# Paged decode attention: the four key blocks of a group on four sets of 32 array columns

## The chip, the cores and the metric

The program runs on one core of one Trainium2 chip. The metric is device time in microseconds for the whole program, the median of the runs; smaller is better. TensorE, VectorE, ScalarE and GpSimd are called PE, DVE, ACT and POOL as in the profile. A matmul holds one operand in the array (the weights, up to 128 columns of them) and streams the other through it; PEld is the loading of the weights.

## What is computed

The program is one inference step of a small decoder: a DeltaNet layer, a latent-attention layer, and an expert layer behind each. The change is in one part of the attention layer, the decode: eight requests, each with one new token, attend over 4096 cached keys that lie in pages. In the reference's terms, for one request (the key's normalising factor `kscale` and the token's own key are folded in by the kernel):

```python
PAST_LEN = 4096; MLA_HEADS = 8; KV_LORA = 256; ROPE_DIM = 64
cache_latent  # pages of (PAGE_SIZE, 256) latents
cache_krope   # pages of (PAGE_SIZE, 64) rotated keys
cache_kscale  # pages of (PAGE_SIZE, 8) per-row per-head factors
# per head h, with the query taken into latent space:
# score[t, h] = (qlat[h] . latent[t] + qrope[h] . krope[t]) * kscale[t, h] * SOFTMAX_SCALE
# p = softmax over the 4096 past tokens and the token itself
# o[h] = sum_t p[t, h] * latent[t]          (256 values, later times w_uv)
```

All of it is float32.

## The kernel before

Everything that matters here is in `mla_dec`. A request's cache is gathered by three indirect DMAs of POOL (line 1651): `c` (the latents, 128 partitions x 32 blocks x 256), `kr` (32 blocks x 64) and `ks`. There are two buffers of each (index `a`), so a gather fills the buffer of the request after the next. The 32 blocks of 128 keys are worked through in eight groups of four (`BQ = 4`, `NG = 8`).

PE's program is written out by hand in `turn` and `step`. Step g of a request does, in this order:

- `flips`: ten 128x128 transposes that turn the latents (lines 1720, 1721) and the rotated keys (line 1725) of group g. ACT and DVE copy the results from PSUM to `cT` and `rT` (lines 1682, 1683, 1903).
- `scores` for group g-1: the weights are the queries, 8 columns wide (`ql`, `qr`), and the streamed operand is `cT` or `rT`. Line 1731 streams all four blocks at once, 512 columns, twice (two halves of the latent); line 1733 streams 256 columns twice. The scores land in `pL` as 8 partitions x 512. DVE copies them to `lines` (line 1851).
- `back` for group g-2: four small transposes (line 1739) bring `lines` into `pS`, keys on partitions.

The softmax of the request before is spread over the steps of this one: `largest`, `over_all`, `lowered`, `summed` and `divided` on DVE, `maximum` and `spread_maximum` on PE, `soften` on ACT. Behind step 4 comes `values` (line 1774): 32 matmuls, the weights `S` 8 columns wide, each streaming 256 columns of `c`, all summed into the same 8 partitions of `pO`. ACT copies them to `vs` (line 1676) in step 6, and `sums` turns them behind step 7 (lines 1779, 1781).

Two waits tie this to the gathers. POOL may refill `c` only when `values` has read it, and PE may start a request only when its latents have landed:

```python
                        apart(pool, at("pv", i - 1, a + 1))
                        gather(a, latents)
...
                    if g == 0:
                        after(pe, (s[f"lc{a}"], i * 16 + 16), (s[f"lr{a}"], i * 16 + 16))
```

The first of these lines stands behind the `kr` and `ks` gathers in POOL's loop. `values` of request r runs in step 4 of request r+1, and it is request r+2 that needs the buffer.

Of the kernel before, what the change touches and what calls it, by code (L numbers as in the profile page):

```python
# [23 lines left out]
ALU = mybir.AluOpType  # L24
ACT = mybir.ActivationFunctionType
AX = mybir.AxisListType
F32 = mybir.dt.float32
U32 = mybir.dt.uint32
ds = bass.ds

P = 128
# [6 lines left out]
H = 8  # L38
# [4 lines left out]
QL, KL, RD = 512, 256, 64  # L43
# [4 lines left out]
PER = PAST // P  # L48
# [9 lines left out]
C_ID, C_ONE, C_UP, C_STRICT, C_NEG, C_LEVEL = 0, 1, 2, 3, 4, 5  # L58
# [149 lines left out]
def part(tile, n, width):  # L208

    dims = " ".join("abcd"[:len(tile.shape) - 1])  # L210
    flat = tile[:].rearrange(f"p {dims} -> p ({dims})") if len(tile.shape) > 2 else tile
    return flat[:, ds(n * width, width)]
# [1360 lines left out]
def mla_dec(core, q, ckvT, krTs, ksc, wuv, os):  # L1573
# [6 lines left out]
    nc = core.nc  # L1580
    N = NS * H
    BQ = 4
    NG = PER // BQ
    T0 = SEQ
    TURNS = NS // 2
    with Marks(core, "pag", inp=96, step=15, turned=1, lat_made=1, self_made=1,
               idx=2, lc0=16, lc1=16, lr0=16, lr1=16, lk0=16, lk1=16,
               flip=2 * NG, half0=2 * NG, half1=2 * NG, keyr=2 * NG, dotted=2 * NG, lined=2 * NG, staged=4, scored=2, soft0=10, soft1=10, maxed=2, spread=2, exped=4,
               pv=2, v_out=2, v_turned=2, o=6, final=1) as s, ExitStack() as ctx:
# [6 lines left out]
        c = [core.sbuf(ctx, "c", [P, PER, KL]) for _ in range(2)]  # L1596
# [3 lines left out]

        qr2 = core.sbuf(ctx, "qr2", [P, NS + 1, 2, H])
        qlat = core.sbuf(ctx, "qlat", [P, 2, NS + 1, H])
        ql = [core.sbuf(ctx, "ql", [P, 2, H]) for _ in range(2)]
        qr = [core.sbuf(ctx, "qr", [P, 2, H]) for _ in range(2)]
        lines = [core.sbuf(ctx, "lines", [H, BQ, P]) for _ in range(2)]
        prod = core.sbuf(ctx, "prod", [P, 3, NS, H])
        spread = core.sbuf(ctx, "spread", [NS, NS, H])
        sself = core.sbuf(ctx, "sself", [P, N])
        krep = core.sbuf(ctx, "krep", [P, N])
        cT = [core.sbuf(ctx, "cT", [P, 2, BQ, P]) for _ in range(2)]  # L1610
        rT = [core.sbuf(ctx, "rT", [P, BQ // 2, P]) for _ in range(2)]
        S = [core.sbuf(ctx, "S", [P, PER, H]) for _ in range(2)]
        m = [core.sbuf(ctx, "m", [P, 6, H]) for _ in range(2)]
        mx = [core.sbuf(ctx, "mx", [H, 1 + H]) for _ in range(2)]
        vs = core.sbuf(ctx, "vs", [H, KL])
        olat = core.sbuf(ctx, "olat", [P, 2, NS, H])
        b0 = [core.psum(ctx, "b0", [P, BQ, P]) for _ in range(2)]
        b1 = [core.psum(ctx, "b1", [P, BQ, P]) for _ in range(2)]
        b2 = core.psum(ctx, "b2", [P, BQ // 2, P])
        pS = core.psum(ctx, "pS", [P, PER, H])  # L1620
        pL = core.psum(ctx, "pL", [P, BQ, P])
        pMO = core.psum(ctx, "pMO", [P, P + 4 * H + KL])
        pM, pO = pMO[:, 0:P + 4 * H], pMO[:, P + 4 * H:]
        M_SPREAD, M_SUM, M_VALUE = (slice(P + k * H, P + (k + w) * H) for k, w in ((0, 1), (1, 1), (2, 2)))

        def flat(tile):
            return tile[:, :, :].rearrange("p a b -> p (a b)")
# [10 lines left out]
        with nc.Block() as block:  # L1638
# [9 lines left out]
            def _(pool):  # L1648
# [9 lines left out]
                with pool.Fori(1, TURNS) as i:  # L1658
                    for a in range(2):
                        apart(pool, at("idx", i, a + 1), at("flip", i - 1, NG * (a + 1)))  # L1660
                        gather(a, keys)
# [5 lines left out]
            @block.scalar  # L1667
            def _(act):
                def soften(i, a):
                    after(act, at(f"soft{a}", i, 7))  # L1670
                    act.activation(S[a][:, :, :], S[a][:, :, :], ACT.Exp).then_inc(s["exped"], 1)
                    act.activation(m[a][:, 3, :], m[a][:, 2, :], ACT.Exp).then_inc(s["exped"], 1)  # L1672

                def value_out(i, a):
                    after(act, at("pv", i, a + 1), at("v_turned", i, a))
                    act.activation(vs[:, :], pO[:H, :], ACT.Copy).then_inc(s["v_out"], 1)

                def turn(i, first):
                    for a in range(2):
                        for g in range(NG):  # L1680
                            after(act, at("flip", i, NG * a + g + 1))
                            act.activation(cT[g % 2][:, 0, :, :], b0[g % 2][:, :, :], ACT.Copy).then_inc(s["half0"], 1)  # L1682
                            act.activation(rT[g % 2][:, :, :], b2[:, :, :], ACT.Copy).then_inc(s["keyr"], 1)
                            if a or not first:
                                if g == 3:
                                    soften(*before(i, a))
                                if g == 6:
                                    value_out(*before(i, a))

                turns(act, turn)  # L1690
                soften(TURNS - 1, 1)
                value_out(TURNS - 1, 1)

            @block.tensor
            def _(pe):
# [4 lines left out]
                for h in range(H):  # L1700
                    pe.transpose(pS[:, h, :], q[:NS, NT, h, QK - P:QK], eye)
                    last = pe.transpose(pS[:RD, H + h, :], q[:NS, NT, h, HD:QK], eye)
                last.then_inc(s["turned"], 1)
                pe.wait_ge(s["step"], 8)
                for h in range(H):
                    for e in range(2):
                        last = pe.matmul(pO[:, e * N + NS * h:e * N + NS * h + NS], wukT[:, h, P * e:P * e + P], qnT[:, h, :], start=True, stop=True)
                last.then_inc(s["lat_made"], 1)
                pe.wait_ge(s["step"], 14)
                own = pS[:, 0:NS, :].rearrange("p b h -> p (b h)")  # L1710
                pe.matmul(own, core.ones, prod[:, 0, :, :].rearrange("p b h -> p (b h)"), start=True, stop=False)
                pe.matmul(own, core.ones, prod[:, 1, :, :].rearrange("p b h -> p (b h)"), start=False, stop=False)
                pe.matmul(own, core.ones[:RD, :], prod[:RD, 2, :, :].rearrange("p b h -> p (b h)"), start=False, stop=True)
                pe.matmul(pM[:, 0:N], core.ones[:NS, :], spread[:, :, :].rearrange("p b h -> p (b h)"), start=True, stop=True).then_inc(s["self_made"], 1)
                pe.wait_ge(s["step"], 16)

                def flips(i, a, g):

# [3 lines left out]
                    if g or a or not isinstance(i, int):  # L1722
                        after(pe, at("keyr", i, NG * a + g))
                    for j in range(BQ // 2):
# [3 lines left out]
                def scores(a, g):  # L1728

                    for e in range(2):  # L1730
                        pe.matmul(pL[:H, :, :].rearrange("p j c -> p (j c)"), ql[a][:, e, :], cT[g % 2][:, e, :, :].rearrange("p j c -> p (j c)"), start=e == 0, stop=False)  # L1731
                    for e in range(2):
                        last = pe.matmul(pL[:H, e:BQ:2, :], qr[a][:, e, :], rT[g % 2][:, :, :], start=False, stop=e == 1)  # L1733
                    last.then_inc(s["dotted"], 1)

                def back(g):

                    for j in range(BQ):
                        last = pe.transpose(pS[:, BQ * g + j, :], lines[g % 2][:, j, :], core.const[:H, C_ID, 0:H])
                    return last  # L1740

                def step(i, a, g, first):

# [27 lines left out]
                def values(i, a):  # L1771
                    after(pe, at("exped", i, 2 * a + 2), at("v_out", i, a))
                    for j in range(PER):
                        last = pe.matmul(pO[:H, :], S[a][:, j, :], c[a][:, j, :], start=j == 0, stop=j == PER - 1)  # L1774
                    last.then_inc(s["pv"], 1)

                def sums(i, a):
                    after(pe, at(f"soft{a}", i, 8), at("v_out", i, a + 1))
                    pe.matmul(pM[:, M_SUM], core.ones, m[a][:, 4, :], start=True, stop=True)
                    for e in range(2):  # L1780
                        last = pe.transpose(pM[:, P + (2 + e) * H:P + (3 + e) * H], vs[:, P * e:P * e + P], core.const[:H, C_ID, 0:H])
                    last.then_inc(s["v_turned"], 1)

                def turn(i, first):
# [15 lines left out]
                for h in range(H):  # L1800
                    for e in range(2):
                        last = pe.matmul(pO[:, NS * h:NS * h + NS], wuv[:, e, HD * h:HD * h + HD], olat[:, e, :, h], start=e == 0, stop=e == 1)
# [3 lines left out]
            def _(dve):  # L1806
                done = [0]

                def then(ins):
                    ins.then_inc(s["step"], 1)  # L1810
                    done[0] += 1
                    dve.wait_ge(s["step"], done[0])
# [5 lines left out]
                then(dve.memset(qr2[:, :, :, :], 0.0))  # L1818
                then(dve.memset(qlat[:, :, :, :], 0.0))
                then(dve.memset(ptf[:, :], 0.0))  # L1820
                dve.wait_ge(s["inp"], 96)
                then(dve.tensor_copy(ptf[:, 0:NS], ptab[:, :]))

# [18 lines left out]

                def stage(v, a):

                    dve.tensor_copy(ql[a][:, :, :], qlat[:, :, ds(v, 1), :].rearrange("p e o h -> p e (o h)")).then_inc(s["staged"], 1)
                    dve.tensor_copy(flat(qr[a]), part(qr2, v, 2 * H)).then_inc(s["staged"], 1)

                def line(i, n):

                    after(dve, at("dotted", i, n))  # L1850
                    dve.tensor_copy(lines[(n - 1) % 2][:, :, :], pL[:H, :, :]).then_inc(s["lined"], 1)  # L1851

                def soft(a, ins):
                    ins.then_inc(s[f"soft{a}"], 1)
# [242 lines left out]
```

## Time and profile before

| what | value |
|---|---|
| median of 3 runs | 4729.99 us (4720.45 to 4735.25) |
| span of the profiled execution | 4702.6 us |
| what lies around the span (median less span) | 27.4 us |
| decode attention in the trace | about 2650 to 3088 us |
| its loop over steps | 2676.5 to 3087.4 us |
| PE busy, whole span | 81% |

The profile gives the span from the first to the last instruction; its execution has no other time of its own, so the metric stands 27.4 us above the span by the median. The share of PE is an average over stages with different limits; the decode attention is one of them, and the rows further down are all from it but the first.

### The profile page before, as it was taken

The numbers are of one execution on the slowest core, as the hardware profiler recorded it, in microseconds if no ns is written. First come the engines' busy times: TensorE is split into PE (matmuls) and PEld (weight loads), VectorE is DVE, ScalarE is ACT, GpSimd is POOL, SyncE is SP. The second block draws the span as 40 slices with busy tenths as digits, with TensorE's granted clock in tenths as the row PEclk, the third lists the DMA queues.
The fourth block names the chain that finished last, engine by engine and source line by source line (L and its number), as shares of the span: only waits on it lengthen the run. The fifth ranks groups of instructions, "written<-read, shape, count | busy, mean of one in ns | idle before, by whom it ended". The sixth has DMA issues, their size and how long they took to land. (4 is left out here: it accounts for less than half of the span.)

```text
span 4702.6 us, 43808 instructions
## 1 busy us (share of the span) xinstructions
PE 3830.8 (81%) x12357; PEld 1998.9 (43%) x12357; DVE 2699.2 (57%) x6392; ACT 951.4 (20%) x2394; POOL 1397.7 (30%) x1188
## 2 busy tenths in 40 slices
PE   7977888788788778787787799987887887877877
PEld 6866674433333333333244544434333333333332
DVE  2423452777777777777334332216777777777773
ACT  2212331121221222212113211102222122121220
POOL 0002340344434444444100000003444444444442
PEclk9987888899989999999799899998999999998988
DMA  2221001899999999999510222217999999999996
GB/s 88 74 57 31 3 1 41 330 392 371 399 371 378 395 381 373 395 376 391 210 52 1 101 102 92 81 40 310 383 371 392 377 371 391 368 379 382 373 387 258
DMA packets 200755, 1207.37 MB, mean 257 GB/s; under 512 B 28936, under 2 KB 48656, under 8 KB 65056
## 3 DMA queue, kind: packets, MB, share of 16 engines
q0 software_dynamic: 152448, 1133.58, 60.3%
q1 hardware_dynamic: 48160, 72.24, 4.6%
q8 instruction: 42, 0.69, 0.1%
q14 instruction: 105, 0.86, 0.0%
HBM read 1197.88 MB, written 7.86 MB: 256 GB/s over the span
## 5 line engine op out<-in xcount | busy, mean ns | idle before, releaser
L1172 PE MATMUL po<-ring,diag 128*128 128x512 f32 x4096 | 2031.2, 650 | 572.8 <-ACT diag L1037 572.4
L994 POOL DMA_INDIRECT ring<-in_uv,idx x1024 | 1226.8, 1198 | 1960.5 <-PE po L1172 1451.0
L1083 DVE SCALAR_TENSOR_TENSOR ring<-ring,xn 128x1024 f32<-128x1024 f32 x1024 | 1224.6, 1224 | 512.4 <-DMA ring<-in_uv,idx 472.4
L1172 PEld LDWEIGHTS po<-ring,diag 128*128 128x128 f32 x4096 | 819.4, 207 | 1612.5 <-issue 953.4
L1032 ACT ACTIVATE hg<-hs 128x4 f32<-128x4 f32 x256 | 52.6, 206 | 1979.6 <-DVE ring L1083 1979.6
L1037 ACT ACTIVATE diag<-gated,hg 128x128 f32<-128x128 f32 x1024 | 327.2, 390 | 15.6 <-ACT hg L1032 8.9
L1132 PE MATMUL pq<-xnT,w 128*128 128x512 f32 (+1 forms) x512 | 260.5, 594 | 1.5 <-ACT q L1012 1.5
L269 PE MATMUL acc<-xnT,w 128*128 128x260 f32 x1024 | 227.9, 385 | 5.1 <-ACT inp L305 4.2
L269 PEld LDWEIGHTS acc<-xnT,w 128*128 128x128 f32 x1024 | 194.8, 191 | 37.7 <-ACT inp L305 6.6
L1059 DVE TENSOR_TENSOR gated<-const,gate 128x2048 f32<-128x2048 f32 x64 | 146.8, 2293 | 2.2
L1133 PEld LDWEIGHTS pqs<-xnT,w 128*128 128x128 f32 x512 | 97.4, 190 | 115.9 <-issue 107.5
L499 POOL TENSOR_TENSOR gU<-const,cols 128x512 f32<-128x512 f32 x8 | 8.4, 1044 | 445.0 <-POOLq L130 418.4
L1903 DVE COPY cT<-b 128x512 f32<-128x512 f32 x64 | 44.3, 692 | 142.7 <-PE b L1725 142.7
L1132 PEld LDWEIGHTS pq<-xnT,w 128*128 128x128 f32 x512 | 90.8, 191 | 82.5 <-issue 82.5
L1731 PE MATMUL pL<-cT,ql 128*8 128x512 f32 x256 | 121.6, 598 | 0.0
L1851 DVE COPY lines<-pL 8x512 f32<-8x512 f32 x64 | 43.5, 679 | 127.7 <-PE pL L1733 127.7
L1774 PE MATMUL pMO<-c,S 128*8 128x256 f32 x512 | 113.5, 383 | 1.3 <-ACT m L1672 1.3
L882 DVE MAX8 sv<-pS 128x8 f32<-128x128 f32 x128 | 31.6, 289 | 136.2 <-issue 88.7
L1483 POOL COPY knh<-kn 128x512 f32 x8 | 4.9, 612 | 334.7 <-SPq L1476 243.6
L1682 ACT ACTIVATE cT<-b 128x512 f32<-128x512 f32 x64 | 38.1, 595 | 322.2 <-PE b L1725 322.2
L1016 ACT ACT_TABLE_LOAD x64 | 82.1, 1283 | 94.5 <-DVE tab L908 92.0
L1075 DVE TENSOR_TENSOR x<-po,x 128x1024 f32<-128x1024 f32 x64 | 78.1, 1221 | 17.5 <-PE po L1172 17.5
(436 smaller groups left out, 4200.4 us busy)
## 6 DMA issues: line engine op xcount, KB each, us to landing
w<-in_w_gdn SPq DMA_DIRECT2D x32, 512.0 KB, 3.5
w<-in_w_peer SPq DMA_DIRECT2D x32, 512.0 KB, 7.8
ring<-in_uv,idx POOLq DMA_INDIRECT x1024, 8.8
S<-in_state_ssm SPq DMA_DIRECT2D x16, 256.0 KB, 3.1
out_ssm_s<-S SPq DMA_DIRECT2D x16, 256.0 KB, 3.2
w<-in_w_gdn_out SPq DMA_DIRECT2D x2, 2048.0 KB, 13.4
w<-in_w_mla_out SPq DMA_DIRECT2D x2, 2048.0 KB, 12.9
wq<-in_w_uq SPq DMA_DIRECT2D x1, 3072.0 KB, 15.5
```

The source lines that it names most:

```text
L269: last = pe.matmul(acc[c % 2][:, r, :], w[:, c, k, :], xnT[:, k, PART * r:PART * r + PART], start=k == 0, stop=k == KD - 1)
L994: pool.indirect_dma_start(out=ring[:, c % RING, :], out_offset=None, in_=uv, in_offset=bass.IndirectOffsetOnAxis(ap=idx[t % 2][:, c:c + 1] ...
L1016: act.activation(k.e[:, :], k.tv[:, :], ACT.Exp, bias=k.low[:, 0:1], accum_out=k.z[:, 0:1]).then_inc(s["exped"], 1)
L1037: act.activation(diag[:, c % RING, :], gated[a][:, c, :], ACT.Copy, scale=hg[a][:, c:c + 1]).then_inc(s["diag"], 1)
L1059: dve.tensor_tensor(gated[b][:, :, :], core.const[:, C_ID:C_ID + 1, :].to_broadcast([P, TOPK, P]), gate[:, :].rearrange("p (c o) -> p c o" ...
L1075: dve.tensor_tensor(core.x[:, t, :], po[t % 2][:, :], core.x[:, t, :], ALU.add).then_inc(s["added"], 1)
L1083: dve.scalar_tensor_tensor(ring[:, c % RING, 0:D], ring[:, c % RING, 0:D], 1.0, xn[:, t, :], ALU.mult, ALU.mult, accum_out=hs[a][:, c:c + ...
L1132: pe.matmul(pq[:, start:], w[:, p, j, :], xnT[:, j, start:SEQ], start=j == 0, stop=j == KD - 1)
L1133: last = pe.matmul(pqs[:, :], w[:, p, j, :], xnT[:, j, SEQ:ROWS], start=j == 0, stop=j == KD - 1)
L1172: last = pe.matmul(po[a][:, HALF * e:HALF * e + HALF], diag[:, c % RING, :], ring[:, c % RING, D + HALF * e:D + HALF * e + HALF], start=c ...
L1731: pe.matmul(pL[:H, :, :].rearrange("p j c -> p (j c)"), ql[a][:, e, :], cT[g % 2][:, e, :, :].rearrange("p j c -> p (j c)"), start=e == 0, ...
L1774: last = pe.matmul(pO[:H, :], S[a][:, j, :], c[a][:, j, :], start=j == 0, stop=j == PER - 1)
```

## The change

`ql` and `qr` become 32 columns wide, with zeros behind the 8 queries. Each of the four blocks of a group gets its own matmul with 128 streamed columns, and its output goes to its own 32 partitions of `pL`, which takes its own 32 columns of the array. `pL` and `lines` are now 128 partitions x 128. The four transposes of `back` become one matmul, with the 128x128 `lines` as weights and 32 columns of the identity streamed. `values` adds blocks 0, 4, 8, ... into partitions 0 to 7, blocks 1, 5, ... into 32 to 39, and so on; `vs` has 128 partitions, and `sums` adds the four parts by a matmul with `pick`, a 0/1 matrix. A setup matmul gives all of `pO` a finite value.

```diff
-        ql = [core.sbuf(ctx, "ql", [P, 2, H]) for _ in range(2)]
-        qr = [core.sbuf(ctx, "qr", [P, 2, H]) for _ in range(2)]
-        lines = [core.sbuf(ctx, "lines", [H, BQ, P]) for _ in range(2)]
+        ql = [core.sbuf(ctx, "ql", [P, 2, COLS]) for _ in range(2)]
+        qr = [core.sbuf(ctx, "qr", [P, 2, COLS]) for _ in range(2)]
+        lines = [core.sbuf(ctx, "lines", [P, P]) for _ in range(2)]
+        pick = core.sbuf(ctx, "pick", [P, COLS])
...
-                    act.activation(vs[:, :], pO[:H, :], ACT.Copy).then_inc(s["v_out"], 1)
+                    act.activation(vs[:, :], pO[:, :], ACT.Copy).then_inc(s["v_out"], 1)
...
+                pe.matmul(pO[:, :], core.ident, core.const[:, C_ID:C_ID + 2, :].rearrange("p a c -> p (a c)"), start=True, stop=True)
...
                     for e in range(2):
-                        pe.matmul(pL[:H, :, :].rearrange("p j c -> p (j c)"), ql[a][:, e, :], cT[g % 2][:, e, :, :].rearrange("p j c -> p (j c)"), start=e == 0, stop=False)
-                    for e in range(2):
-                        last = pe.matmul(pL[:H, e:BQ:2, :], qr[a][:, e, :], rT[g % 2][:, :, :], start=False, stop=e == 1)
+                        for j in range(BQ):
+                            pe.matmul(pL[COLS * j:COLS * j + COLS, :], ql[a][:, e, :], cT[g % 2][:, e, j, :], start=e == 0, stop=False)
+                    for j in range(BQ):
+                        last = pe.matmul(pL[COLS * j:COLS * j + COLS, :], qr[a][:, j % 2, :], rT[g % 2][:, j // 2, :], start=False, stop=True)
...
-                    for j in range(BQ):
-                        last = pe.transpose(pS[:, BQ * g + j, :], lines[g % 2][:, j, :], core.const[:H, C_ID, 0:H])
-                    return last
+                    return pe.matmul(pS[:, BQ * g:BQ * g + BQ, :], lines[g % 2][:, :],
+                                     core.ident.rearrange("p (j c) -> p j c", c=COLS)[:, :, 0:H], start=True, stop=True)
...
                     for j in range(PER):
-                        last = pe.matmul(pO[:H, :], S[a][:, j, :], c[a][:, j, :], start=j == 0, stop=j == PER - 1)
+                        b = COLS * (j % BQ)
+                        last = pe.matmul(pO[b:b + H, :], S[a][:, j, :], c[a][:, j, :], start=j < BQ, stop=j >= PER - BQ)
...
                     for e in range(2):
-                        last = pe.transpose(pM[:, P + (2 + e) * H:P + (3 + e) * H], vs[:, P * e:P * e + P], core.const[:H, C_ID, 0:H])
+                        last = pe.matmul(pM[:, P + (2 + e) * H:P + (3 + e) * H], vs[:, P * e:P * e + P], pick[:, 0:H], start=True, stop=True)
...
+                for a in range(2):
+                    then(dve.memset(ql[a][:, :, :], 0.0))
+                    then(dve.memset(qr[a][:, :, :], 0.0))
+                then(dve.tensor_reduce(pick[:, :], core.ident.rearrange("p (j c) -> p c j", c=COLS), AX.X, ALU.add))
...
-                    dve.tensor_copy(lines[(n - 1) % 2][:, :, :], pL[:H, :, :]).then_inc(s["lined"], 1)
+                    dve.tensor_copy(lines[(n - 1) % 2][:, :], pL[:, :]).then_inc(s["lined"], 1)
```

On PE, at the end of a step 4, the order of before is this. A row gives the line, the output and the inputs, the output's shape, and how often it follows in a row; `pMO` holds `pO`.

```order
L1725 MATMUL b_313<-const,kr 128x128 x2
L1731 MATMUL pL<-cT,ql 8x512 x2
L1733 MATMUL pL<-rT,qr 8x2x128 x2
L1739 MATMUL pS<-const,lines 128x8 x4
L1774 MATMUL pMO<-c,S 8x256 x32
L1720 MATMUL b_310<-const,c 128x128
```

The same place of the changed program, where the line numbers have moved by three or four:

```order
L1728 MATMUL b_314<-const,kr 128x128 x2
L1735 MATMUL pL<-cT,ql 32x128 x8
L1737 MATMUL pL<-rT,qr 32x128 x4
L1742 MATMUL pS<-const,lines 128x32
L1778 MATMUL pMO<-c,S 8x256 x32
L1723 MATMUL b_311<-const,c 128x128
```

Nothing stands in another place than before: four score matmuls have become twelve shorter ones, four transposes one matmul, and the 32 of `values` are as many and as long as they were.

## Rows read from the trace of the kernel before

**Rows 1.** The page: span and busy time of the engines.

```profile
span 4702.6 us, 43808 instructions
PE 3830.8 (81%) x12357; PEld 1998.9 (43%) x12357; DVE 2699.2 (57%) x6392; ACT 951.4 (20%) x2394; POOL 1397.7 (30%) x1188
```

**Rows 2.** Stage windows: window, us, busy time by engine, granted clock, DMA share, GB/s.

```profile
2880.00:2930.00 50.00, 49.19 (x250) 22.85 (x249) 14.59 (x32) 7.62 (x19) 2.82 (x3) 1.00 0.28 107
```

**Rows 3.** Groups by line from 2676 to 3090 us: busy, mean ns | idle before.

```profile
L1731 PE MATMUL pL<-cT,ql 128*8 128x512 f32 x256 | 121.6, 598 | 0.0
L1774 PE MATMUL pMO<-c,S 128*8 128x256 f32 x512 | 113.5, 383 | 1.3 <-ACT m L1672 1.3
L1733 PE MATMUL pL<-rT,qr 128*8 128x256 f32 x256 | 65.7, 379 | 0.0
L1739 PE MATMUL pS<-const,lines 8*128 8x8 f32 x256 | 26.3, 207 | 0.4 <-DVE lines L1851 0.4
```

**Rows 4.** Timeline of one step: start, us, engine, line, operation.

```profile
2861.86 0.33 PE L1720 MATMUL b<-const,c 128*128 128x128 f32 x1
2862.79 0.38 PE L1725 MATMUL b<-const,kr 128*128 128x128 f32 x2
2863.11 1.88 PE L1731 MATMUL pL<-cT,ql 128*8 128x512 f32 x4
2863.54 0.09 PEld L1731 LDWEIGHTS pL<-cT,ql 128*8 128x8 f32 x1 [0.34 <-issue]
2863.71 0.38 ACT L1683 ACTIVATE rT<-b 128x256 f32<-128x256 f32 x1
2864.83 1.03 PE L1733 MATMUL pL<-rT,qr 128*8 128x256 f32 x4
2865.78 0.41 PE L1739 MATMUL pS<-const,lines 8*128 8x8 f32 x4
2865.89 0.68 DVE L1851 COPY lines<-pL 8x512 f32<-8x512 f32 x1 [1.98 <-PE pL L1733]
2866.12 0.33 PE L1720 MATMUL b<-const,c 128*128 128x128 f32 x1
```

**Rows 5.** Timeline from values to the next request's first transpose.

```profile
2785.75 8.15 PE L1774 MATMUL pMO<-c,S 128*8 128x256 f32 x37
2793.83 0.33 PE L1720 MATMUL b<-const,c 128*128 128x128 f32 x1
...
2806.61 0.39 PE L1779 MATMUL pMO<-m,const 128*128 128x8 f32 x2
2806.93 0.29 PE L1781 MATMUL pMO<-const,vs 8*128 8x8 f32 x2
...
2807.79 0.33 PE L1720 MATMUL b<-const,c 128*128 128x128 f32 x1 [0.57 <-DMA c<-in_cache_latent,idx]
```

**Rows 6.** POOL's timeline: first and last of six latent gathers.

```profile
2745.10 0.94 POOL L1651 DMA_INDIRECT c<-in_cache_latent,idx  x1 [25.31 <-PE pMO L1774]
...
2993.56 0.94 POOL L1651 DMA_INDIRECT c<-in_cache_latent,idx  x1 [25.32 <-PE pMO L1774]
```

**Rows 7.** Waits, 2676 to 3090 us: total us, times, longest.

```profile
PE b L1720 <- DMA c<-in_cache_latent,idx: 5.2, 6, 1.1
```

**Rows 8.** Timeline and a window behind a clock drop.

```profile
3007.15 0.33 PE L1720 MATMUL b<-const,c 128*128 128x128 f32 x1 [1.05 <-DMA c<-in_cache_latent,idx]
3008.98 2.93 PE L1731 MATMUL pL<-cT,ql 128*8 128x512 f32 x4
...
3009.00:3011.00 2.00, 2.00 (x4) 0.35 (x4) 0.69 (x1) 0.87 (x2) 0.00 (x0) 0.50 0.00 0
```

**Rows 9.** Timeline: first step, and the last values.

```profile
2659.01 0.17 DVE L1822 CAST ptf<-ptab 128x8 f32<-128x8 int32 x1 [7.64 <-DMA wukT<-in_w_ukT]
2676.53 0.45 PE L1720 MATMUL b<-const,c 128*128 128x128 f32 x1 [3.44 <-DMA kr<-in_cache_krope,idx]
...
3065.35 15.67 PE L1774 MATMUL pMO<-c,S 128*8 128x256 f32 x64 [1.34 <-ACT m L1672]
```

More of the change, by code:

```diff
@@ L1582, in mla_dec @@
     BQ = 4
+    COLS = P // BQ
     NG = PER // BQ
@@ L1585, in mla_dec @@
     TURNS = NS // 2
-    with Marks(core, "pag", inp=96, step=15, turned=1, lat_made=1, self_made=1,
+    with Marks(core, "pag", inp=96, step=17, turned=1, lat_made=1, self_made=1,
                idx=2, lc0=16, lc1=16, lr0=16, lr1=16, lk0=16, lk1=16,
@@ L1614, in mla_dec @@
         mx = [core.sbuf(ctx, "mx", [H, 1 + H]) for _ in range(2)]
-        vs = core.sbuf(ctx, "vs", [H, KL])
+        vs = core.sbuf(ctx, "vs", [P, KL])
         olat = core.sbuf(ctx, "olat", [P, 2, NS, H])
@@ L1620, in mla_dec @@
         pS = core.psum(ctx, "pS", [P, PER, H])
-        pL = core.psum(ctx, "pL", [P, BQ, P])
+        pL = core.psum(ctx, "pL", [P, P])
         pMO = core.psum(ctx, "pMO", [P, P + 4 * H + KL])
@@ L1703, in _ @@
                 last.then_inc(s["turned"], 1)
-                pe.wait_ge(s["step"], 8)
+                pe.wait_ge(s["step"], 13)
                 for h in range(H):
@@ L1708, in _ @@
                 last.then_inc(s["lat_made"], 1)
-                pe.wait_ge(s["step"], 14)
+                pe.wait_ge(s["step"], 19)
                 own = pS[:, 0:NS, :].rearrange("p b h -> p (b h)")
@@ L1714, in _ @@
                 pe.matmul(pM[:, 0:N], core.ones[:NS, :], spread[:, :, :].rearrange("p b h -> p (b h)"), start=True, stop=True).then_inc(s["self_made"], 1)
-                pe.wait_ge(s["step"], 16)
+                pe.wait_ge(s["step"], 21)
+                pe.matmul(pO[:, :], core.ident, core.const[:, C_ID:C_ID + 2, :].rearrange("p a c -> p (a c)"), start=True, stop=True)
                 def flips(i, a, g):
@@ L1843, in stage @@
                 def stage(v, a):
-                    dve.tensor_copy(ql[a][:, :, :], qlat[:, :, ds(v, 1), :].rearrange("p e o h -> p e (o h)")).then_inc(s["staged"], 1)
-                    dve.tensor_copy(flat(qr[a]), part(qr2, v, 2 * H)).then_inc(s["staged"], 1)
+                    dve.tensor_copy(ql[a][:, :, 0:H], qlat[:, :, ds(v, 1), :].rearrange("p e o h -> p e (o h)")).then_inc(s["staged"], 1)
+                    dve.tensor_copy(qr[a][:, :, 0:H], qr2[:, ds(v, 1), :, :].rearrange("p o e h -> p (o e) h")).then_inc(s["staged"], 1)
                 def line(i, n):
                     after(dve, at("dotted", i, n))
-                    dve.tensor_copy(lines[(n - 1) % 2][:, :, :], pL[:H, :, :]).then_inc(s["lined"], 1)
+                    dve.tensor_copy(lines[(n - 1) % 2][:, :], pL[:, :]).then_inc(s["lined"], 1)
                 def soft(a, ins):
```

## Prediction

> **What bounds it now.** I read the page first: PE is busy for 81% of the span [rows 1]. That is an average, so I turned to the decode attention, the only place that the change touches. In its windows PE is busy for 49.2 of 50 us at full clock (1.00, which is 2.4 GHz), while DMA moves data for 28% of the time [rows 2]. The groups by line show on what: lines 1731, 1774 and 1733 keep PE for 301 of the 414 us that the view covers [rows 3]. All three have weights only 8 columns wide, so most of the array has nothing to do in them. Those are the matmuls that the change spreads over the array.
>
> A step of four blocks repeats every 4.26 us (2861.86 to 2866.12) [rows 4]. Its parts, from start to start: ten transposes 1.25, line 1731 1.72, line 1733 0.95, `back` 0.34. The reader is to see two more things there. Each float32 matmul leaves two records with a load each (256 records of line 1731 for 128 matmuls, two in each of 64 steps), and a record of 512 columns takes 1.72 / 4 = 0.43 us: so 0.107 us for each 128 columns. And between the last transpose (2862.79 plus one pitch of 0.11 is 2862.90) and the first score matmul (2863.11) lie 0.21 us where the pitch of a transpose is 0.11: 0.10 us is lost where the array changes from 128 columns to a narrow set. `values` is 64 records of 256 columns, with a pitch of (8.15 - 0.38) / 36 = 0.216 us, 13.8 us for one request [rows 3, 5].
>
> The second limit is right behind PE. `values` ends at about 2793.83 with the first transpose behind it, and only then may POOL issue the gather that refills those latents [rows 5]. PE does three more steps and `sums`, and then waits 0.57 us for it [rows 5]; over the six such places it waits 5.2 us in all, 0.87 each [rows 7]. The gather fits almost exactly into three steps of today's length. From `values` to the next request's start it takes 13.96 + 0.30 = 14.26 us on average, whatever PE does. Six requests have this wait; they come (2993.56 - 2745.10) / 5 = 49.7 us apart [rows 6].
>
> **The change part by part.** Scores: 12 matmuls of 128 columns, 24 records of 0.107 us. If nothing overlaps that is 2.57 us, as now. If the four column sets run fully at once, it is 0.64. No row of this trace shows two sets at work together, so these are the bounds, and a third value lies between. The two records of one matmul go to the same columns, one behind the other, and the second has to wait until the first has streamed. If matmuls start in program order, the next block's first record can only overlap this second one. Then each matmul costs one record: 12 + 1 records, 1.39 us. I take this middle value, since all records of the trace start in order. With the 0.10 us of the change of shape that is 1.49 in place of 2.67.
>
> The Trainium skill ("TensorE: Matmul & The Clock Gate", Part 3: Packing small matmuls) has a measured 2.38x for three column tiles, and says that matmuls start and end strictly in program order. By its rate, carried on to four tiles (an estimate: 2.57 / 3.2), the scores would take about 0.8 us; by its order rule with two records to a tile, the 1.39 above. No run here shows either yet.
>
> A floor of issue is possible too: four pairs of load and matmul take 0.41 us in line 1739 with 0.207 for one, a pitch of 0.068 us [rows 3, 4]. With 128-column loads that would make 24 pairs 1.63 us; loads of 32 columns should be shorter, so it bounds the middle value from above and takes most of the difference between it and the best case away.
>
> `back`: two records with a 128-column load. The nearest row is line 1779, two such records, 0.32 us to the next line [rows 5]. In place of 0.34, no change. A step is then 1.25 + 1.49 + 0.32 = 3.06 us: 1.20 less.
>
> `values`: 32 matmuls, one record each exposed, 33 x 0.216 = 7.1 us in place of 13.8, 6.7 less (bounds: 64 / 4 records, 3.5 us, and nothing). `sums` gets two more records of line 1779's kind, 0.3 us a request [rows 5].
>
> DVE's copy of the scores reads 128 columns instead of 512, so it falls from 0.68 us towards 0.3 [rows 4]; that is off the path. A shorter step must still cover the copies: ACT's end at 2863.71 + 0.38 = 2864.09, 1.2 us behind the last transpose's start, and the next step's transposes of the keys and its scores need them some 2.7 us behind it, still in time [rows 4]. The setup's five DVE instructions stand ahead of a wait of 7.64 us for a DMA, and the extra matmul on `pO` ahead of PE's 3.44 us for the first keys [rows 9]; uncovered they would cost some 2 us once.
>
> Now the gather. Three steps and `sums` are 3 x 3.06 + 0.9 = 10.1 us, but the gather needs 14.26: PE waits 4.2 us at each of six requests. The period becomes 14.26 + 5 x 3.06 + 7.1 + 0.5 (the softmax's small matmuls, what is left of 49.7 by the same sum now) = 37.2 us. An idle PE also loses its clock. Once after a wait of 1.05 us it fell to 0.50 (1.2 GHz): the transposes took 1.83 us (3007.15 to 3008.98) instead of 1.25, and line 1731 2.93 instead of 1.88, 1.6 us lost; the last `values`, behind several short waits, took 15.67, 1.9 more than 64 x 0.216 [rows 4, 8, 9]. I add 1.8 us to each period: 39.0, or 10.7 us less than 49.7.
>
> The sum: six periods 64; from the first transpose (2676.53) to the first gather 13 steps and one `values`, 13 x 1.20 + 6.7 = 22; behind the last period four steps' worth of scores and the last `values`, 4 x 1.20 + 6.7 = 12 [rows 6, 9]. Together 98 us, less 1 for `sums` and setup: 97. The span goes from 4702.6 to 4606; with the 27.4 us around it, 4633 against the median of 4730. If PE alone set the end it would be 64 x 1.20 + 8 x 6.7 = 130; the gathers and the clock keep 33 back.
>
> **The rivals.**
>
> Full overlap: the column sets take two records each without holding up the rest. Step 2.31 us, `values` 3.5; period 14.26 + 11.6 + 3.5 + 0.5 + 1.8 = 31.6, 18 less; 6 x 18 + 13 x 1.95 + 10.3 + 4 x 1.95 + 10.3 = 162, so 4568. For it: nothing in the trace forbids it. Against: the two records of a matmul, and the 0.068 us pitch of pairs.
>
> No overlap: float32 matmuls run one after another wherever they land. Columns streamed are as many as now (512 x 2 + 256 x 2 a step; 256 x 32 in `values`), so the time stays: 4730, within 5 us. The step-by-step widths agree with it as well as with the others, since before only one set was ever used.
>
> Slower, by the price of changing columns: if the array must drain or load in the open each time the column set changes, as it does between 128 columns and 8, each of the 12 score matmuls and 32 of `values` costs 0.10 us more [rows 4]. That is 1.2 us a step and 3.2 a request, 64 x 1.2 + 8 x 3.2 = 102 less the 5.2 us of waits that it covers: 4827. It decides against the change from about 0.1 us on if nothing overlaps. What speaks against it is that a load runs under the matmul ahead of it (2863.54, within line 1731's run) [rows 4]. The skill's same section says that a load overlaps a running matmul only if its rows of the array differ; all rows are the same here, and by it each of 24 records would show its load of 0.09 us, 2.1 us a step. The row just named speaks against it.
>
> Also slower: with PE waiting each period and the matmuls thinner, the clock could stay at 1.2 GHz. The step would be 6.1 us and the request 63, not 49.7, some 90 us more. Transposes at the stage's start brought it up, so I give it little.
>
> **How the numbers follow.** Middle overlap 0.43, full 0.27, none 0.14, dear column changes 0.10, clock 0.06. About 0.3%, 14 us, is what a measurement of this kernel can tell from no change. Both overlap cases are faster by far, and of "none" a little may be; faster 0.72, same 0.13, slower 0.15. The range reaches from full overlap to no change, 4562 to 4738; between the overlap cases alone it would be 4562 to 4650.
>
> **What would show it.** In the profile after: line 1735's records start about 0.05 us apart in mean (0.107 for two) if the middle case holds, 0.03 if full, 0.107 if none; a step of 3.06 us; `values` of 7.1; "DMA c" as the wait of six first transposes, 4 us each, with the gather still taking 14.3 us from `values` to the next transpose, and the clock under 1.00 behind each. It is wrong if the steps come 4.2 us apart, if loads stand in the open between the matmuls, or if the latent waits are short although the steps are: then the gather is faster than I think.

## The result and the profile after

The changed kernel takes 4565.08 us (median of four runs, 4561.73 to 4570.19) against 4730.56 us for the one before. The ratio of the runs is 0.9667, with a 95% interval of 0.9651 to 0.9683: 165 us, or 3.3%, less. That lies in my range of 4562 to 4738, but only 3 us above its lower end and 68 us below its likeliest point of 4633; it is at the rival "full overlap", which I had put at 4568.

The page of the changed kernel, its span and the engines' busy time, stands against [rows 1]:

```profile
span 4568.4 us, 45641 instructions
PE 3653.2 (80%) x13271; PEld 1977.5 (43%) x13271; DVE 2677.0 (59%) x6397; ACT 951.9 (21%) x2394; POOL 1396.5 (31%) x1188
```

PE's share has hardly moved, and PE has 914 more matmul records. (A record is one load of weights with its matmul; a float32 matmul leaves two, a transpose one.) The page does not show where the time went; the step does. The timeline of one step of the changed kernel answers to [rows 4]:

```profile
2795.75 0.31 PE L1723 MATMUL b<-const,c 128*128 128x128 f32 x1
2796.66 0.38 PE L1728 MATMUL b<-const,kr 128*128 128x128 f32 x2
2796.97 0.64 PE L1735 MATMUL pL<-cT,ql 128*32 128x128 f32 x16
2797.43 0.40 PE L1737 MATMUL pL<-rT,qr 128*32 128x128 f32 x8
2797.76 0.41 PE L1742 MATMUL pS<-const,lines 128*128 128x32 f32 x2
2797.90 0.29 DVE L1859 COPY lines<-pL 128x128 f32<-128x128 f32 x1
2798.01 0.31 PE L1723 MATMUL b<-const,c 128*128 128x128 f32 x1
```

A step repeats every 2.26 us (4.26 before). The transposes still take 1.22. The scores take 0.79 from their first record to `back`, where they took 2.67: 24 records of 0.107 us in 0.69 us, with 0.10 for the change of array shape. That is 6.4 record times where four records at a time would need 6. The same row cut short shows how they start. In a window that ends at 2797.065, then in one that ends at 2797.17:

```profile
2796.97 0.32 PE L1735 MATMUL pL<-cT,ql 128*32 128x128 f32 x4
...
2796.97 0.43 PE L1735 MATMUL pL<-cT,ql 128*32 128x128 f32 x8
```

Four records have started in the first 0.1 us (a window that ends at 2797.00 already has all four, within 0.03 us), and the next four end 0.11 us behind them: bursts of four, one record time apart.

The changed kernel's timeline from `values` to the next request answers to [rows 5], its waits to [rows 7], POOL's latent gathers to [rows 6], and a window behind the wait to [rows 8]:

```profile
2789.90 3.64 PE L1778 MATMUL pMO<-c,S 128*8 128x256 f32 x64
2793.47 0.33 PE L1723 MATMUL b<-const,c 128*128 128x128 f32 x1
...
2808.74 0.45 PE L1723 MATMUL b<-const,c 128*128 128x128 f32 x1 [7.66 <-DMA c<-in_cache_latent,idx]
...
2812.51 0.31 PE L1723 MATMUL b<-const,c 128*128 128x128 f32 x1
```

```profile
PE b L1723 <- DMA c<-in_cache_latent,idx: 42.4, 6, 8.0
```

```profile
2727.14 0.94 POOL L1653 DMA_INDIRECT c<-in_cache_latent,idx  x1 [9.46 <-PE pMO L1778]
...
2890.67 0.94 POOL L1653 DMA_INDIRECT c<-in_cache_latent,idx  x1 [9.28 <-PE pMO L1778]
```

```profile
2807.00:2811.00 4.00, 2.26 (x10) 2.00 (x10) 0.00 (x0) 0.00 (x0) 0.00 (x0) 0.50 0.50 211
```

`values` takes 3.6 us instead of 13.8, again a quarter. PE now stands idle for 42.4 us at six places where it waited 5.2, and each time resumes at a granted clock of 0.50 (1.2 GHz): the first step behind this wait takes 3.77 us (2808.74 to 2812.51). This is the mildest of the six. Behind the next wait the clock is still at 0.50 when the second step runs:

```profile
2839.88 0.48 PE L1723 MATMUL b<-const,c 128*128 128x128 f32 x1 [6.57 <-DMA c<-in_cache_latent,idx]
...
2842.00:2845.00 3.00, 3.00 (x33) 2.35 (x32) 0.98 (x2) 0.87 (x2) 0.00 (x0) 0.50 0.00 0
```

Requests come (2890.67 - 2727.14) / 5 = 32.7 us apart, 17.0 less than before.

I take the stage from the start of the first latent gather to the end of the last copy, `os`, which takes 0.2 us. First the kernel before, then the changed one:

```profile
2659.85 0.96 POOL L1651 DMA_INDIRECT c<-in_cache_latent,idx  x1 [39.42 <-DVE idx L1816]
...
L1920 DVE COPY os<-pMO x1: 225/225/225, 3087.4 to 3087.4; 128x64 f32<-128x64 f32 x1
```

```profile
2675.63 0.97 POOL L1653 DMA_INDIRECT c<-in_cache_latent,idx  x1 [39.35 <-DVE idx L1820]
...
L1928 DVE COPY os<-pMO x1: 224/224/224, 2946.9 to 2946.9; 128x64 f32<-128x64 f32 x1
```

The changed kernel needs 271.5 us (2675.63 to 2947.1), the one before 427.8 (2659.85 to 3087.6). The stage gives 156 us. The two profiled spans differ by only 134, because parts that the change does not touch took 22 us longer in this execution: decode began 16 us later, and what follows the stage took 6 us more. The medians differ by 9 us more than the stage. Parts like these vary by as much from one execution to the next, but what the 9 us are was not traced.

### The profile page after: what moved, and what is told of

Its sections match the earlier page's. It is cut to its first block and busy times, and to the rows that moved or that the text cites. A ratio compares the mean times of both kernels' runs of the same rounds, so it can differ in the third digit from the quotient of the medians.

```text
span 4568.4 us, 45641 instructions
## 1 busy us (share of the span) xinstructions
PE 3653.2 (80%) x13271; PEld 1977.5 (43%) x13271; DVE 2677.0 (59%) x6397; ACT 951.9 (21%) x2394; POOL 1396.5 (31%) x1188
## 5 line engine op out<-in xcount | busy, mean ns | idle before, releaser
L1032 ACT ACTIVATE hg<-hs 128x4 f32<-128x4 f32 x256 | 52.6, 205 | 2002.6 <-DVE ring L1083 2002.6
L1037 ACT ACTIVATE diag<-gated,hg 128x128 f32<-128x128 f32 x1024 | 327.1, 390 | 15.6 <-ACT hg L1032 8.9
L882 DVE MAX8 sv<-pS 128x8 f32<-128x128 f32 x128 | 31.6, 289 | 136.6 <-issue 93.2
L1723 PE MATMUL b<-const,c 128*128 128x128 f32 x256 | 69.9, 307 | 44.2 <-DMA c<-in_cache_latent,idx 42.4
L640 DVE TENSOR_TENSOR U<-pB,U 128x512 f32<-128x512 f32 x48 | 33.2, 692 | 90.4 <-PE pB L548 90.4
L830 DVE TENSOR_TENSOR x<-bank,x 128x512 f32<-128x512 f32 x16 | 11.1, 692 | 125.6 <-PE bank L819 125.6
L1083 DVE DVE_READ_ACCUMULATOR ring<-ring,xn 128x1 f32 x1024 | 83.6, 82 | 0.0
```

The lines of the kernel that those rows point to most:

```text
L1032: act.activation(hg[a][:, GRP_C * g:GRP_C * g + GRP_C], hs[a][:, GRP_C * g:GRP_C * g + GRP_C], ACT.Gelu).then_inc(s["gelu"], 1)
L1037: act.activation(diag[:, c % RING, :], gated[a][:, c, :], ACT.Copy, scale=hg[a][:, c:c + 1]).then_inc(s["diag"], 1)
L1083: dve.scalar_tensor_tensor(ring[:, c % RING, 0:D], ring[:, c % RING, 0:D], 1.0, xn[:, t, :], ALU.mult, ALU.mult, accum_out=hs[a][:, c:c + ...
L1723: pe.transpose(b0[g % 2][:, j, :], c[a][:, BQ * g + j, 0:P], core.ident)
```

## The experiments

All are on the changed kernel unless said otherwise. Times are medians beside runs of the kernel before on the same chip; a stage time is read from the trace as just above. The ratio to the kernel before has its 95% interval where there were several runs.

### How deep the overlap goes: the order of the column sets

The changed kernel goes to another column set with every matmul. I kept the work and changed only the order in `values` and `scores`, so that runs of 2, 4 or 8 matmuls (4, 8 or 16 records) go to one set:

```diff
-                    for j in range(PER):
+                    for j in (BQ * k + b for o in range(0, PER // BQ, L) for b in range(BQ) for k in range(o, o + L)):
                         b = COLS * (j % BQ)
...
-                    for e in range(2):
-                        for j in range(BQ):
+                    for j in range(BQ):
+                        for e in range(2):
                             pe.matmul(pL[COLS * j:COLS * j + COLS, :], ql[a][:, e, :], ...)
-                    for j in range(BQ):
                         last = pe.matmul(pL[COLS * j:COLS * j + COLS, :], qr[a][:, j % 2, :], ...)
```

With L = 2, and all three matmuls of a block together in `scores`:

> The changed kernel with another order on PE: in values, two matmuls in a row go to the same column set before the next set (four records in a row), and in scores the three matmuls of a block stand together (six records in a row). In the changed kernel values take 3.57 us and the scores of a step 0.79 us, with records starting in bursts of four. Theory 'short queue': records leave in program order, and each column set holds one record that streams and one that waits; two records of one matmul then cost nothing, but four in a row hold up the others. It expects values of 7.0 us, scores of 2.0 us, and some 4640 us in all. Theory 'independent sets': however long the run, a set does not hold up another: 3.6 us, 0.8 us, 4565 us. My prediction's theory of strict order with no waiting place would have had the changed kernel itself at 7 us and is out.

With L = 8, and in `scores` only the two latent matmuls of a block together:

> As the one before, with longer and shorter runs: in values, eight matmuls in a row per set (16 records), in scores the two latent matmuls of a block together (four records), the key matmuls interleaved as in the changed kernel. Short queue: a set's 16 records let the next one in only when 14 have streamed, so values take (3 x 14 + 16) x 0.216 = 12.5 us, scores about 1.4 us, and the whole some 4655 us. Independent sets: 3.6 us, 0.8 us, 4565 us. A deeper but finite queue would show between: full speed at two matmuls in a row and less at eight.

Measured: 4602.5 us and 4623.9 us (one run each), with stages of 307.6 and 335.0 us against the changed kernel's 271.5. The timeline of the first, a step's scores and one `values`:

```profile
2797.75 0.65 PE L1735 MATMUL pL<-cT,ql 128*32 128x128 f32 x6
2798.21 0.27 PE L1736 MATMUL pL<-rT,qr 128*32 128x128 f32 x1
2798.24 0.30 PE L1735 MATMUL pL<-cT,ql 128*32 128x128 f32 x2
2798.32 0.27 PE L1736 MATMUL pL<-rT,qr 128*32 128x128 f32 x1
2798.35 0.30 PE L1735 MATMUL pL<-cT,ql 128*32 128x128 f32 x2
2798.46 0.27 PE L1736 MATMUL pL<-rT,qr 128*32 128x128 f32 x1
2798.49 0.30 PE L1735 MATMUL pL<-cT,ql 128*32 128x128 f32 x2
...
2799.26 0.41 PE L1741 MATMUL pS<-const,lines 128*128 128x32 f32 x2
...
2809.05 3.66 PE L1777 MATMUL pMO<-c,S 128*8 128x256 f32 x64
```

And of the second:

```profile
2795.34 0.67 PE L1735 MATMUL pL<-cT,ql 128*32 128x128 f32 x16
2795.80 0.42 PE L1737 MATMUL pL<-rT,qr 128*32 128x128 f32 x8
2796.16 0.41 PE L1742 MATMUL pS<-const,lines 128*128 128x32 f32 x2
...
2803.83 11.42 PE L1778 MATMUL pMO<-c,S 128*8 128x256 f32 x64
```

Both theories missed. Four records in a row on one set cost next to nothing (`values` 3.66 us, scores 0.82), where the short queue expected half speed. Six in a row nearly double the scores (1.51 us), and sixteen in a row give 11.42 us, where independent sets expected no change. What fits is the short queue with a larger number: records leave in program order, and a set takes up to K of them, one that streams and K - 1 that wait. I count `values` in record times of 0.216 us, the pitch of [rows 5]. The 0.38 us of the last record hold its own streaming, so the count is (11.42 - 0.38) / 0.216 + 1 = 52.1 for sixteen in a row. K = 4 gives 52, K = 3 gives 55, K = 5 gives 49. (The next expectation counts with 0.2135 and without the 1, hence its 51.7; the choice of K does not hang on it.) For the scores with six in a row K = 4 gives 12 record times, K = 3 gives 15 and K = 5 gives 9; 1.51 less 0.10 is 13.2, nearest to K = 4 but a tenth above it.

The first row of the first fence shows the same thing in another way. In the program the key matmul of block 0 (line 1736) stands behind four records of line 1735 only. In the trace six records of line 1735 have started before it, and block 0 has only four: two are of a later block. So records of different sets do not start in program order; those of one set do, by this model. K = 4 also gives the order of the whole step as the trace has it: six latent records, then one key record and two latent ones in turn, four times, and towards the end one and one.

A rival is a waiting room that all sets share: the four oldest records that have not started may start in any order across sets. Worked out in the same way it gives 52 for sixteen in a row and 13 for the scores with six, as good as the model. But it gives 19 for `values` with four in a row, where (3.66 - 0.38) / 0.216 + 1 = 16.2 was measured, and 9 for the scores of the second run, where 0.82 less 0.10 is 6.7. The model gives 16 and 6. So each set has its own places, as far as these two pictures go.

The model had now been fitted to these runs, so I let it forecast one more, L = 4:

> The changed kernel with four matmuls of values in a row per column set (eight records), scores as in the changed kernel. A small model is put to the test here: records leave in program order, and a set takes up to K of them, one that streams and K - 1 that wait; a record of values streams for 0.2135 us. With K = 4 it gives 16 record times for values with one or two matmuls in a row, 52 with eight, and 12 for the scores with three in a row, and the runs so far showed 16, 16, 51.7 and 13. For four in a row it gives 36 record times with K = 4, 7.9 us for values with the latency of the last; K = 3 gives 43 (9.4 us), K = 5 gives 29 (6.4 us). If the hold-up at eight had another cause (a limit in the number of instructions looked at in all, say 64), four in a row would still run at 16, 3.6 us.

```profile
2794.86 8.00 PE L1778 MATMUL pMO<-c,S 128*8 128x256 f32 x64
```

(8.00 - 0.38) / 0.216 + 1 = 36.3 record times, against 36 for K = 4, 43 for K = 3 and 29 for K = 5. A limit on all records together that first bites at sixteen in a row would have left 3.6 us, and is out. The whole took 4595.2 us (one run), the stage 304.7.

### Two column sets instead of four

```diff
-                        b = COLS * (j % BQ)
-                        last = pe.matmul(pO[b:b + H, :], S[a][:, j, :], c[a][:, j, :], start=j < BQ, stop=j >= PER - BQ)
+                        b = COLS * (j % 2)
+                        last = pe.matmul(pO[b:b + H, :], S[a][:, j, :], c[a][:, j, :], start=j < 2, stop=j >= PER - 2)
```

`sums` reads only the 64 partitions of these two sets.

> The changed kernel, with values on two column sets instead of four (blocks alternate between sets 0 and 1); scores as in the changed kernel. If the gain is the number of sets that stream at once, values take half of the 13.8 us of before, 7.0 us, and the whole about 27 us more than the changed kernel, 4592 us. If the bursts of four records were the two records of each of two matmuls side by side, so that only two sets ever work together, values stay at 3.6 us and the whole at 4565 us.

Measured: 4580.6 us (one run), and in the timeline:

```profile
2790.67 7.08 PE L1778 MATMUL pMO<-c,S 128*8 128x256 f32 x64
```

7.08 us, half of one set's 13.8 and twice four sets' 3.64: the gain is the number of sets that stream at once, and the bursts of four are four sets. The total is 16 us above the changed kernel where 27 was expected, but a single total says little about that, with an expert layer that varies by as much. The stage says more: 297.7 us (2671.17 to 2968.9), 26 above the changed kernel's.

### Each half of the change alone

`scores_only` has line 1774, `vs` and `sums` as before, `values_only` has lines 1731 to 1739 and `lines` as before.

> Only scores and back on column sets; values, vs and sums as before the change. The steps are 2.26 us, values 13.8. Theory 'the gather covers three of eight steps': of the 2.0 us saved in a step only five of eight in a period count, since the three behind values are waited off against the gather, and the cold clock takes 1.8 us back: six periods 8.2 us shorter, the first part 26, the end 8, in all 83 us less than before: about 4645 us. Rival: the two parts share the gain in proportion to PE time saved (128 of 210 us for the scores), so 100 us less: 4628 us.

> Only values, vs and sums on column sets; scores and back as before the change. Steps 4.26 us, values 3.6. The 10.2 us saved lie outside the stretch that the gather covers, so they count in full eight times, 82 us, and nothing is lost to the clock: about 4646 us, and the waits for latents stay near 5 us. By the rival of shares in proportion (82 of 210 us of the 165 gained) it would be 65 us less: 4663 us.

Measured: 4639.09 us (0.9828, 0.9803 to 0.9854) and 4639.03 us (0.9829, 0.9800 to 0.9857). The stage takes 354.7 and 352.0 us, 73 and 76 less than before. First the waits and the first and last gather of `scores_only`, then the same of `values_only`:

```profile
PE b L1723 <- DMA c<-in_cache_latent,idx: 43.8, 6, 7.9
...
2737.89 0.94 POOL L1653 DMA_INDIRECT c<-in_cache_latent,idx  x1 [19.77 <-PE pMO L1777]
...
2949.98 0.94 POOL L1653 DMA_INDIRECT c<-in_cache_latent,idx  x1 [19.59 <-PE pMO L1777]
```

```profile
PE b L1723 <- DMA c<-in_cache_latent,idx: 6.8, 6, 2.2
...
2756.92 0.94 POOL L1653 DMA_INDIRECT c<-in_cache_latent,idx  x1 [15.01 <-PE pMO L1778]
...
2958.25 0.94 POOL L1653 DMA_INDIRECT c<-in_cache_latent,idx  x1 [15.01 <-PE pMO L1778]
```

Both parts are worth about the same: their ratios differ by far less than their intervals are wide, and the stages by 3 us. That is so although the scores save 8 x 2.0 = 16 us of PE a request and `values` only 10.2. Of the scores' gain the wait eats three steps: the waits of the full change, 42.4 us, are all there with the scores alone (43.8) and not with `values` alone (6.8). `values` lies outside the stretch that the gather covers and counts in full. That is the first theory; the shares in proportion (4628 and 4663) would put the two 35 us apart, and the medians are 0.1 us apart. Both stage gains are some 6 to 10 us smaller than I expected: the periods fell by 7.3 and 9.4 us instead of 8.2 and 10.2.

### The gather out of the way: a third latent buffer

```diff
-        c = [core.sbuf(ctx, "c", [P, PER, KL]) for _ in range(2)]
+        c = [core.sbuf(ctx, "c", [P, PER, KL]) for _ in range(3)]
...
-                        apart(pool, at("idx", i, a + 1), at("flip", i - 1, NG * (a + 1)))
+                        after(pool, at("idx", i, a + 1), at("pv", 0, 2 * i + a - 2))
+                        latent(2 * i + a)
+                        after(pool, at("flip", i - 1, NG * (a + 1)))
                         gather(a, keys)
...
-                        apart(pool, at("pv", i - 1, a + 1))
-                        gather(a, latents)
```

> The changed kernel with a third buffer for the latents: the gather of a request's latents starts a whole request earlier, in the step 4 of the request two before it. For the room the last row tile of q is kept in a small tile (one more copy, some 2 us), and the loop over turns is written out. Theory 'gather and clock keep it back': the 42.4 us of waits for latents and the clock lost behind them go, the period falls from 32.7 us to PE's own 8 x 2.26 + 3.6 + 1.0 = 22.7 us, six times 10 us: 4505 to 4515 us. Rival: the DMA engines or DVE and ACT are the next limit just behind (5.4 MB of gathers in 22.7 us), so that new waits take over and the time stays above 4535 us.

Measured: 4501.29 us, ratio to the kernel before 0.9535 (0.9507 to 0.9563). Its stage windows and its first and last gathers in steady state:

```profile
2760.00:2800.00 40.00, 40.00 (x641) 30.84 (x640) 19.65 (x54) 13.69 (x34) 5.27 (x6) 1.00 0.53 207
```

```profile
2725.51 0.94 POOL L1660 DMA_INDIRECT c<-in_cache_latent,idx  x1 [9.97 <-PE pMO L1790]
...
2817.13 0.94 POOL L1660 DMA_INDIRECT c<-in_cache_latent,idx  x1 [9.97 <-PE pMO L1790]
```

No wait for latents is left, PE is busy for 40.0 of 40 us at a granted clock of 1.00, and requests come (2817.13 - 2725.51) / 4 = 22.9 us apart, PE's own 22.7. The control has the written-out loop and the kept tile of `q`, but two buffers:

> The control for three_buffers: the changed kernel with the loop over turns written out and the last tile of q kept apart, but with its two latent buffers and the gathers in their old order. If three_buffers owes its 64 us to the earlier gather, this stays at the changed kernel's time, 4565 us within some 10 us (two executions of this program differ by as much in its expert layers), with six waits for latents of 7 us each. If the written-out loop or the freed room is what helped, it comes down to some 4500 us.

It took 4550.47 us (0.9628, 0.9610 to 0.9647), with 39.3 us of waits and a stage of 267.3 us; with three buffers the stage is 214.7. So the earlier gather is worth 52.6 us in the stage, 49 in the medians and 44 by the ratios: the control's waits, 39.3, and some 13 that are left for the cold clock, 2.2 at each wait. The control is 15 us below the changed kernel (18 by the ratios), of which the stage shows 4; where the rest comes from I did not find. The last of this group puts the third buffer into the kernel before:

> The kernel before with the third latent buffer (and the kept tile of q and the written-out loop). If the gather is nearly covered before the change, the 5.2 us of waits and one drop of the clock (1.6 us) go and the copy costs some 2: 5 us less, not to be told from the kernel before. If three buffers help by themselves, by anything else than the waits (less overlap of DMA with the rest, say), it would be faster by some tens of us as the changed kernel was with them (64 us).

4708.02 us, 0.9972 (0.9957 to 0.9986), a stage of 424.9 us instead of 427.8, and requests 48.8 us apart instead of 49.7. It gains a little, 13 us by the ratio, of which 3 are in the stage. The same buffer that is worth some 50 us behind the change is worth little ahead of it.

## Why the prediction came out as it did

- **What bounds it**: right. The stage was PE's, and the latents' gather stood right behind it. All the waits that the change uncovered are at the one place named, six times: 42.4 us against my 25 for the middle case and, by the same sum, 14.26 - 3 x 2.31 - 0.9 = 6.4 each or 39 for full overlap.
- **The scores**: the step that failed. I took "the next block's first record can only overlap this second one", 12 + 1 records and 1.49 us with the change of shape. Measured: 0.79. The ground for it, that all records start in order, came from a trace in which only one column set was ever used, so it said nothing about several. The runs put this in its place: a set takes four records, and the two of one float32 matmul hold up nothing. The step went to 2.26, not 3.06; `values` to 3.6, not 7.1. The other estimate that I had set beside it, about 0.8 us for the scores, was close to the 0.69 (0.79 with the change of shape), and I gave it too little weight.
- **The rule on order**: the Trainium skill ("TensorE: Matmul & The Clock Gate", Part 3: Packing small matmuls) says that matmuls start strictly in program order. Here line 1736 starts behind records that follow it in the program, so the measurement decides against the rule for several column sets. Its other rule, that a load overlaps a running matmul only if the rows differ, fails as well: 16 loads and matmuls on the same 128 rows start within 0.46 us, in bursts of four with no gap for the loads.
- **The floor of issue**: no limit. I held that pairs of load and matmul could not come closer than 0.068 us or a little less. They come 0.69 / 24 = 0.029 us apart.
- **`back`, copies, setup**: as costed. `back` takes 0.25 us instead of my 0.32, DVE's copy 0.29, and neither the copies nor the setup show as a new wait of PE.
- **The gather and the clock**: right in kind, a little small in size. I had PE resume 14.26 us behind `values`. It is 14.7 in the mean of the six places, from 13.8 to 15.6 (15.27 in the one shown, 2793.47 to 2808.74). POOL now issues the keys' gather 5.8 us behind the latents' instead of 9.8, and the median landing of the latents went from 13.3 to 13.7 us; that the one causes the other was not tried. The cold clock cost 1.5 us in the place first shown, but more at the others. From where PE resumes to the next latent gather the changed kernel takes 17.8 us there (2808.74 to 2826.57) and 18.7 in the mean of five; three_buffers, at full clock, takes 16.3 (2800.80 to 2817.13). That is 2.4 us a period against my 1.8. My figure rested on one place: I laid its fall of the clock to the 1.05 us wait ahead of it, but the trace of the kernel before has a wait of 1.11 us at 2957.26 behind which the clock stays at 1.00. The period of the full case came to 32.7 us where I had 31.6.
- **The sum**: the full case forecast 162 us, the stage shows 156, and the medians 165. The agreement of 4568 with 4565 is better than the terms deserve, and that the measured time lies inside my range at all is owed to the range, which reached down to full overlap, not to the case that I forecast. I also took the 27.4 us between span and median as what lies around the span; the profiled run of the changed kernel took 4570.19 us with a span of 4568.4, so only 1.8 us lie around it, and most of the 27 was a difference between executions. It shifted nothing, since I subtracted from both.
- **The rivals on the other side**: no dear column change (bursts of four are free of gaps), no clock stuck at 1.2 GHz (three_buffers runs at 1.00 from 2720 to 2840 us of its span).
- **The chances**: I gave the full overlap 0.27 and the middle case 0.43. The trace held nothing for the middle one beyond a picture of the array. Between two bounds with no row in between, the forecast should have leaned less on it.

## What to carry to other kernels

A matmul whose weights are at most 32 columns wide leaves room for three more beside it: four of them on four column sets took about a quarter of the time, as long as no set got more than four records (two float32 matmuls) in a row before the next set had its turn. When a stage is shortened, subtract from each period only what lies outside the stretch that a transfer covers: here five of eight steps and all of `values`. And look then at the transfer: the buffer that was worth a few microseconds before the change was worth some 50 behind it, and it made the fastest version, 4501 us.

## What the runs showed that I had not expected

- Each column set takes four records, one streaming and three waiting: 16, 16, 36 and 52 record times by the model for runs of 1, 2, 4 and 8 matmuls in `values`; measured (3.64, 3.66, 8.00 and 11.42 us, less 0.38, over 0.216, plus 1) 16.1, 16.2, 36.3 and 52.1. Only the last but one of these was forecast; the model was fitted to the others.
- Pairs of a 32-column load and a 128-column float32 matmul ran 0.029 us apart in mean, four sets together, without a gap for the loads.
- PE resumed at 1.2 GHz behind each of six waits of 6.2 to 8.0 us. The clock came back within the first step in one place and within the second in the others, so a wait cost 2.4 us of clock in the mean of five, not the 1.5 of the mildest.
- Parts of the program that no kernel here changed differ by some 10 to 16 us between executions (the stage began at 2659.85 us in one trace and at 2675.63 in the next, and DVE's first instruction of the decode, ahead of all that the change adds, already stood at 2650.78 and 2666.62), so single runs of such kernels say little about 15 us; the stage's own rows do.
